# Differential attention: GpSimd combines the softmax pair of the last 256 of 768 keys, VectorE the first 512

## Chip, cores, metric

One NeuronCore of a Trainium2 chip runs the whole kernel in one launch. The metric is the device time of that launch in microseconds (us), lower is better. Names of engines: PE is TensorE (PEld its weight load), DVE is VectorE, ACT is ScalarE, POOL is GpSimd, SP is SyncE.

## What is computed

The model is two blocks in a row: a two-layer recurrent and attention block, and then two hybrid layers over 512 latent tokens and 256 context tokens. Each hybrid layer has three branches; the change is in the first, differential attention. Cut to what matters:

```python
def diff_attn_dense(q, k, v, lam):
    s = jnp.einsum('bqhcd,bkhcd->bhcqk', q, k).astype(jnp.float32) * (q.shape[-1] ** -0.5)
    p = jax.nn.softmax(s, axis=-1)
    a = (p[:, :, 0] - lam * p[:, :, 1]).astype(v.dtype)
    return jnp.einsum('bhqk,bkhv->bqhv', a, v)
```

There are 4 heads. Each has two score maps (c = 0 and 1) with 64 channels each, whose softmaxes are subtracted, the second times lam. A latent query sees all 768 keys, a context query the 256 context keys.

## The kernel before

The kernel is written engine by engine: each engine has one program that walks through the same list of stages, and semaphores, named in the code, order them. Nothing is rescheduled, so the order within an engine is the order of the code.

The stage `da` (differential attention) comes once in each of the two hybrid layers. It is cut into jobs. A latent job is one head and one block of 128 queries: two score maps of 128 x 768. A context job is one head and both context blocks: four maps of 128 x 256. Layer 0 has 20 jobs (for each head four latent ones, then one of context), layer 1 has 16, all latent; so 32 are latent and 4 of context. A job n passes through:

1. PE, `scores` (L986 latent, L977 context): q times k into three PSUM banks, 0 to 2 for even jobs and 3 to 5 for odd.
2. DVE, `maxima` (L2392): the negated row maxima, from PSUM.
3. ACT, `exps` (L1674): exponentials into the SBUF buffer `DE[:, n % 2]`, with row sums.
4. DVE, `probs`: reciprocals of the sums (L2401), the ratio r (L2404, one column), and then one SCALAR_TENSOR_TENSOR (L2410), e0 = e1 * r + e0, over 768 columns for a latent job, two of 256 for a context job. The common factor 1/sum is left out and put in at step 7.
5. PE, `transposes`: blocks 0 to 3 of e0 (L1001) into bank 6, then, for latent jobs, blocks 4 and 5 (L1006) into bank 7. Ahead of blocks 4 and 5 PE waits on `da_evac` of job n-1, since bank 7 also holds that job's output.
6. ACT, `evac` (L1683, L1687): the transposed blocks to SBUF. PE, `values` (L1020): times v into bank 7.
7. DVE, `evac` (L2418): bank 7 times the reciprocal, to SBUF, which gives `da_evac`.
8. ACT `squares` (L1695 to L1702), DVE `scale` (L2427), PE `turn` (L1029), DVE `post` (L2432): norm, transposition back and gate, once for each head (and again for its context rows).

The order within a turn n of the loop is: PE scores(n+2), values(n-1), transposes(n), turn(n-2); DVE probs(n), post(n-3), maxima(n+2), evac(n-1), scale(n-2); ACT exps(n+1), evac(n), squares(n-1). Two lines at the loop's end prepare the next stage's first weights (L575 on DVE, ahead of the loop, and L594 to L596 on PE behind it). GpSimd has nothing to do in `da`: before, it went from the two loads of the rotary tables (L2925) to a wait on `da_y`, the stage's last result, ahead of the load of `wg_in` (L2929). Elsewhere it issues loads, and in the stage `mlstm` it computes masks (L2824) and queries (L2833).

The program has a limited number of semaphores. Three that the change touches: `lru_w` counted the eight loads of `LRUW` (L2877); `loaded_pool` counted the load of `ROT` (L2872) and is waited for in `wait_loaded`, which DVE calls before L1965 and PE before its `lru` stage; `ml_w` told the exponential of the rows `WQ` (L1455) to the GpSimd stores of `wrow` (L2939).

Of the kernel before, what the change touches and what calls it, by code (L numbers as in the profile page):

```python
# [11 lines left out]
ALU = mybir.AluOpType  # L12
# [237 lines left out]
def build(nc, x, ctx_in, w8, wb, wm, wf_in, wg_in, params, rows, lru_w, sgu_w, sgu_b, rope, rot, nbias, vlat, mrow, wrow,  # L250
# [203 lines left out]
    def pc(name, i=0):  # L454
# [7 lines left out]
    slot_uses = [len(range(k, n_ml, 4)) for k in range(4)]  # L462
    state_uses = [len(range(k, n_lat, 4)) for k in range(4)]
    in_layer0 = dict(
        da_probs=n_da, da_evac=n_da, da_o=n_da, da_max=n_da, da_half=16, da_scaled=8, da_turned=8, da_rs=8, da_y=8,
        ml_s=n_mu, ml_u=2 * n_lat, ml_c0=n_lat, ml_c=3 * n_lat, ml_masked=n_ml, ml_qs=n_lat, decay=n_ml,
        ml_zm=n_ml, ml_o=n_ml, ml_dens=n_mu, ml_divf=n_mu, ml_divb=n_mu, ml_rs=n_mu, ml_scaled=n_mu,
        ml_turned=n_mu, ml_y=n_mu, ml_w=1, ml_stored=64, ml_rows=1, ml_l=1, ml_ac=1, ml_emc=1,
        bz_silu=6, cv_done=4, gate_mm=2, gate_f=2, gate_cols=2, wg_hi=1, wg_lo=1, wg_loaded=16, bqk=8, cv_scaled=8, rope_loaded=32,
        rope_done=8, na_probs=2 * n_na, na_max=n_na, na_values=n_na, v_stored=16 * 8, v_blocks=16 * 7,  # L470
        **{f"ml_bm{k}": 16 * slot_uses[k] for k in range(4)}, **{f"ml_bw{k}": 16 * state_uses[k] for k in range(4)})
# [22 lines left out]
    def wait_loaded(eng):  # L494

        eng.wait_ge(loaded, 16)
        eng.wait_ge(sem("rows_loaded"), 16)
        for half in x_loaded:
            eng.wait_ge(half, 16)
        eng.wait_ge(loaded_pool, 16)  # L500

    def wait(eng, s, v):

# [257 lines left out]

    def pe_lru(pe, st):

        pe.wait_ge(sem("lru_w"), 16 * 8)
        for m in range(4):
            wait_free(pe, st, m, 0)
        for m in range(4):
            for g in range(2):
                b = (2 * m + g) % 4
                wait_free(pe, st, b, m // 2)  # L770
                pe.matmul(PS[:, b, :], LRUW[:, 4 * g + m, :], XA[:, m, :],
                          start=True, stop=True).then_inc(full[b], 1)
# [193 lines left out]
    def pe_da(pe, st):  # L966
        ly, jobs = st.layer, st.jobs
        nj = len(jobs)

        def scores(j):  # L970
            n, h, p = j["n"], j["h"], 3 * (j["n"] % 2)
            wait_free(pe, st, p, n // 2)
            lo, hi = slice(0, 64), slice(64, 128)
            if j["ctx"]:
                for qb in range(2):
                    for c, r in ((0, lo), (1, hi)):
                        mm = pe.matmul(PS[:, p + c, qb * TC:(qb + 1) * TC], Q[r, h, T + qb * P:T + (qb + 1) * P],  # L977
                                       K[r, h, T:TA], start=True, stop=True, skip_group_check=True)
            else:
                q0 = P * j["qb"]  # L980
                half = sem("da_half")
                for i, (r, b, c0, k0, k1) in enumerate(((lo, p + 1, 0, T, TA), (hi, p + 2, 0, TC, TA),
                                                        (lo, p, 0, 0, T), (hi, p + 1, TC, 0, TC))):
                    if i == 3:
                        pe.wait_ge(half, past("da_half", ly) + sum(not k["ctx"] for k in jobs[:n]) + 1)
                    mm = pe.matmul(PS[:, b, c0:c0 + k1 - k0], Q[r, h, q0:q0 + P], K[r, h, k0:k1], start=True,  # L986
                                   stop=True, skip_group_check=True)
                    if i == 0:
                        mm.then_inc(half, 1)
            mm.then_inc(full[p], 1)  # L990

        def transposes(j):
            n = j["n"]
            pe.wait_ge(sem("da_probs"), past("da_probs", ly) + n + 1)
            wait_free(pe, st, 6, n)
            outs = sum(i["last"] for i in jobs[:max(n - 2, 0)])
            wait(pe, sem("da_y"), past("da_y", ly) + outs)
            e = DE[:, n % 2, :]
            for i in range(4):
                o = i if not j["ctx"] else 2 * (i % 2) + i // 2  # L1000
                mm = pe.transpose(PS[:, 6, o * P:(o + 1) * P], e[:, i * P:(i + 1) * P], IDENT[:, :])  # L1001
            mm.then_inc(full[6], 1)
            wait(pe, sem("da_evac"), past("da_evac", ly) + n)
            if not j["ctx"]:
                for i in range(4, 6):
                    mm = pe.transpose(PS[:, 7, (i - 4) * P:(i - 3) * P], e[:, i * P:(i + 1) * P], IDENT[:, :])  # L1006
                mm.then_inc(full[7], 1)

        def values(j):
            n, h = j["n"], j["h"]  # L1010
            nl = sum(not i["ctx"] for i in jobs[:n + 1])
            pe.wait_ge(freed[6], st["free", 6] + n + 1)
            pe.wait_ge(freed[7], st["free", 7] + nl)
            wait(pe, sem("da_evac"), past("da_evac", ly) + n)
            at = DAT[n % 2]
            for qb in range(1 + j["ctx"]):
                tiles = (4, 5) if j["ctx"] else range(6)
                for i, t in enumerate(tiles):
                    o = i * TC + qb * P if j["ctx"] else i * P
                    mm = pe.matmul(PS[:, 7, qb * P:(qb + 1) * P], at[:, o:o + P], V[:, t, h * P:(h + 1) * P],  # L1020
                                   start=i == 0, stop=i == len(tiles) - 1, skip_group_check=True)
            mm.then_inc(sem("da_o"), 1)

        def turn(j):

            pe.wait_ge(sem("da_scaled"), past("da_scaled", ly) + j["g"] + 1)
            pe.wait_ge(freed[6], st["free", 6] + min(j["n"] + 3, nj))
            for i in range(2 if j["ctx"] else 4):
                mm = pe.transpose(PS[:, 6, i * P:(i + 1) * P], DO[:, j["g"] % 2, i * P:(i + 1) * P], IDENT[:, :])  # L1029
            mm.then_inc(sem("da_turned"), 1)  # L1030

        pe.wait_ge(sem("rope_done"), past("rope_done", ly) + 8)
        for b in range(8):
            wait_free(pe, st, b, 0)
        scores(jobs[0])
        scores(jobs[1])
        for n in range(nj + 2):
            if n + 2 < nj:
                scores(jobs[n + 2])
            if 0 <= n - 1 < nj:  # L1040
                values(jobs[n - 1])
            if n < nj:
                transposes(jobs[n])
            else:
                pe_head(pe, st.merge, n - nj)
            if 0 <= n - 2 < nj and jobs[n - 2]["last"]:
                turn(jobs[n - 2])
        if st.merge.ctx:
            pe_head(pe, st.merge, 2)
# [343 lines left out]
    def act_units(act, own, st):  # L1393
# [4 lines left out]
        for u, ev in enumerate(st.evs):  # L1398
# [46 lines left out]
            elif ev in ("bq", "bk"):  # L1445
# [5 lines left out]
                if ev == "bk":  # L1451
                    act_gates(act, own, st)
                else:
                    act.wait_ge(sem("ml_rows"), past("ml_rows", st.layer) + 1)
                    act.activation(WQ[0:8, :, :], WQ[0:8, :, :], ACT.Exp).then_inc(sem("ml_w"), 1)  # L1455
                for m in range(4):
                    w = 4 * (8 * st.layer + c0 + m)
                    wait_unit(act, st, u, m, st.ctx)
# [920 lines left out]
    def dve_da(dve, own, st):  # L2379
# [3 lines left out]
        def sums(j, i, at=16):  # L2383
            c = at + 4 * (j["n"] % 4) + i
            return SMALL[:, c:c + 1]
# [9 lines left out]
        def probs(j):  # L2395
            n, p = j["n"], 3 * (j["n"] % 2)
            e = DE[:, n % 2, :]
            dve.wait_ge(freed[p], st["free", p] + n // 2 + 1)
            nq, w = (2, TC) if j["ctx"] else (1, TA)
            c = 4 * (n % 4)  # L2400
            own.link(dve.reciprocal(SMALL[:, 64 + c:64 + c + 2 * nq], SMALL[:, 16 + c:16 + c + 2 * nq]))  # L2401
            for i in range(nq):
                r = SMALL[:, 32 + 4 * (n % 2) + i:33 + 4 * (n % 2) + i]
                own.mark(dve.scalar_tensor_tensor(out=r, in0=sums(j, i), scalar=sums(j, nq + i, 64),  # L2404
                                                  in1=LAM[:, ly, 1:2], op0=ALU.mult, op1=ALU.mult))
            own.wait()
            for i in range(nq):
                r = SMALL[:, 32 + 4 * (n % 2) + i:33 + 4 * (n % 2) + i]
                e0, e1 = e[:, i * w:(i + 1) * w], e[:, (nq + i) * w:(nq + i + 1) * w]
                ins = dve.scalar_tensor_tensor(out=e0, in0=e1, scalar=r, in1=e0, op0=ALU.mult, op1=ALU.add)  # L2410
            ins.then_inc(sem("da_probs"), 1)

# [443 lines left out]
    def _(pool):  # L2856
# [17 lines left out]
        for g in range(2):  # L2874
            for half in range(2):
                for q in range(2):
                    pool.dma_start(LRUW[64 * half:64 * half + 64, 4 * g + 2 * q:4 * g + 2 * q + 2,  # L2877
                                        64 * half:64 * half + 64],
                                   lru_w[g, half, :, 2 * q:2 * q + 2, :]).then_inc(sem("lru_w"), 16)
        pool.wait_ge(w_ready[1], 16)  # L2880
        for i in range(2):
            pool.dma_start(mod_slab(i), wm[i, :, :, :]).then_inc(mod_loaded[i], 16)
        for st in stages:
# [50 lines left out]
                    pool.dma_start(mrow[st.layer, 4 * d:4 * d + 4, :], m_[4 * d:4 * d + 4, :]).then_inc(  # L2934
                        sem("ml_stored"), 16)
            if st.kind == "units" and "bo" in st.evs:
                pool.wait_ge(sem("ml_w"), past("ml_w", st.layer) + 1)
                for d in range(2):
                    pool.dma_start(wrow[st.layer, 4 * d:4 * d + 4, :], WQ[4 * d:4 * d + 4, d, :]).then_inc(  # L2939
                        sem("ml_stored"), 16)  # L2940
# [8 lines left out]
                pool_queries(pool, next_st, next_st.passes[0])  # L2949
            if st.kind == "mlstm":  # L2950
                pool_mlstm(pool, st)

            def bias(ly, i):

# [202 lines left out]
```

## Time and profile before

| | |
|---|---|
| median of 3 runs | 3112.86 us (3111.77 to 3113.13) |
| the profiled execution: its time, its span | 3115.25 us, 3113.5 us |
| busy: PE / DVE / ACT / POOL | 96% / 48% / 37% / 5% of the span |
| stage `da`, layer 0 (first scores to the last `values`) | 1371.9 to 1459.9 us |
| stage `da`, layer 1 | 2413.1 to 2486.0 us |
| chain that ended last, by engine | PE 84%, DVE 9%, ACT 3% |

The profile's busy share is an average over the whole program; the two `da` stages are 161 us of it. In them neither PE nor DVE is busy all the time, so the chain of waits (followed back from the last instruction to what released each step) is what tells which instruction's length counts. Times in the rows further down are us from the span's start.

### The profile page before, as it was taken

What the parts mean: (1) busy time and instruction counts of PE and PEld (TensorE: products, weight loads), DVE (VectorE), ACT (ScalarE), POOL (GpSimd) and SP (SyncE); (2) the same over time, 40 slices, a digit from 0 to 9 for tenths busy, and PEclk for the clock granted to TensorE, in tenths of its full rate; (3) what the DMA queues carried; (4) which work ended last, traced back from release to release, by engine and by line L of the source; (5) the groups of instructions that cost most, each with busy time, mean ns of one, the idle gap of its engine ahead of it and who ended that gap; (6) DMA issues with size and microseconds to landing.
All of it is one profiled execution on the core that took longest, in us unless ns stands there. A gap on an engine that the chain in (4) does not pass through costs nothing.

```text
span 3113.5 us, 38501 instructions
## 1 busy us (share of the span) xinstructions
PE 2975.4 (96%) x15486; PEld 2424.6 (78%) x15486; DVE 1497.5 (48%) x2136; ACT 1155.9 (37%) x1828; POOL 147.6 (5%) x206
## 2 busy tenths in 40 slices
PE   7999999999999998989999999999999899999998
PEld 5767888777788887867888878868877678888776
DVE  4645454645454657267252542263444735353454
ACT  4335233425352344136233331163221634251352
POOL 1000000010000000000000400100000000120100
PEclk9999999999999999999999999999999999999999
DMA  4232322331332221110211211211111022222322
GB/s 178 95 142 101 122 108 101 113 122 68 109 107 91 97 90 54 68 48 4 74 42 62 90 67 54 95 59 61 54 61 68 21 77 67 90 88 81 112 75 81
DMA packets 44460, 256.79 MB, mean 82 GB/s; under 512 B 6344, under 2 KB 6352, under 8 KB 20512
## 3 DMA queue, kind: packets, MB, share of 16 engines
q1 hardware_dynamic: 30528, 204.30, 18.5%
q0 software_dynamic: 13792, 50.51, 5.0%
q8 instruction: 102, 1.67, 0.2%
q14 instruction: 38, 0.31, 0.0%
HBM read 250.51 MB, written 4.28 MB: 82 GB/s over the span
## 4 chain that ended last, share of the span: by engine, by line
PE 84%; DVE 9%; ACT 3%; issue 1%; DMA 1%; POOL 1%; DVEq 0%; SPq 0%; ACTq 0%
PE PS L805 13%; PE PS L806 13%; PE PS L807 13%; PE PS L786 7%; PE PS L785 7%; PE PS L787 7%; PE PS L751 2%; PE PS L750 2%; PE PS L749 2%; DVE SMALL L2392 2%; PE PS L986 1%; DMA W<-in_w 1%; PE PS L698 1%; PE PS L594 1%; PE PS L596 1%
## 5 line engine op out<-in xcount | busy, mean ns | idle before, releaser
L805 PE MATMUL PS<-HHX,WHX 128*128 128x512 f32 (+1 forms) x1456 | 511.2, 351 | 9.9 <-DVE WLX L2242 7.0
L806 PE MATMUL PS<-HL,WHX 128*128 128x512 f32 (+1 forms) x1456 | 512.3, 352 | 0.0
L1559 ACT ACTIVATE WHX<-W 128x2048 fp32r<-128x2048 f32 (+1 forms) x102 | 174.6, 1712 | 578.9 <-DMA W<-in_w 391.3
L807 PE MATMUL PS<-HHX,WLX 128*128 128x512 f32 (+1 forms) x1024 | 357.6, 349 | 0.0
L2242 DVE TENSOR_TENSOR WLX<-W,WHX 128x2048 fp32r<-128x2048 f32 x60 | 137.5, 2292 | 383.4 <-ACT WHX L1559 383.4
L805 PEld LDWEIGHTS PS<-HHX,WHX 128*128 128x128 f32 x1456 | 278.8, 191 | 48.4 <-DVE WLX L2242 7.8
L806 PEld LDWEIGHTS PS<-HL,WHX 128*128 128x128 f32 x1456 | 277.5, 191 | 36.6
L786 PE MATMUL PS<-HL,WH 128*128 128x512 f32 x672 | 265.4, 395 | 0.0
L785 PE MATMUL PS<-HH,WH 128*128 128x512 f32 x672 | 263.3, 392 | 0.0
L2242 DVE TENSOR_TENSOR WL<-W,WH 128x2048 fp32r<-128x2048 f32 x68 | 155.9, 2292 | 221.7 <-ACT WH L1559 221.6
L787 PE MATMUL PS<-HH,WL 128*128 128x512 f32 x672 | 261.7, 389 | 0.0
L1559 ACT ACTIVATE WH<-W 128x2048 fp32r<-128x2048 f32 x68 | 130.3, 1916 | 282.4 <-PE PS L787 252.1
L807 PEld LDWEIGHTS PS<-HHX,WLX 128*128 128x128 f32 x1024 | 196.0, 191 | 24.7
L2280 DVE SCALAR_TENSOR_TENSOR ARENA<-PS,PC,ARENA 128x511 f32<-128x511 f32 (+1 forms) x176 | 131.6, 748 | 73.1 <-ACT ARENA L1587 60.0
L2242 DVE TENSOR_TENSOR WLM<-W,WHX 128x1024 fp32r<-128x1024 f32 (+1 forms) x42 | 70.6, 1680 | 179.2 <-ACT WHX L1559 179.1
L807 PE MATMUL PS<-HHX,WLM 128*128 128x512 f32 (+1 forms) x432 | 154.9, 359 | 0.0
L785 PEld LDWEIGHTS PS<-HH,WH 128*128 128x128 f32 x672 | 125.8, 187 | 30.8
L787 PEld LDWEIGHTS PS<-HH,WL 128*128 128x128 f32 x672 | 126.1, 188 | 28.2
L786 PEld LDWEIGHTS PS<-HL,WH 128*128 128x128 f32 x672 | 126.2, 188 | 27.2
L749 PE MATMUL PS<-WHX,HHX 128*128 128x512 f32 x288 | 119.6, 415 | 0.0
L751 PE MATMUL PS<-WHX,HL 128*128 128x512 f32 x288 | 112.7, 391 | 0.0
L750 PE MATMUL PS<-WLX,HHX 128*128 128x512 f32 x288 | 112.5, 391 | 0.0
(533 smaller groups left out, 5902.4 us busy)
## 6 DMA issues: line engine op xcount, KB each, us to landing
W<-in_w SPq DMA_DIRECT2D x172, 1024.0 KB, 4.7
XC<-in_wm POOLq DMA_DIRECT2D x12, 1024.0 KB, 5.1
H<-in_wm POOLq DMA_DIRECT2D x12, 1024.0 KB, 5.7
W<-in_wb SPq DMA_DIRECT2D x24, 512.0 KB, 3.2
W<-in_w SPq DMA_DIRECT2D x8, 768.0 KB, 4.1
ARENA<-mrow POOLq DMA_DIRECT2D x12, 256.0 KB, 4.1
ARENA<-wrow POOLq DMA_DIRECT2D x12, 256.0 KB, 4.6
PR<-in_nbias POOLq DMA_DIRECT2D x12, 256.0 KB, 2.9
```

The costliest lines, as they stand in the source:

```text
L749: pe.matmul(PS[:, t, :], xh, wh[:, s, c], start=s == 0 and k == 0, stop=False)
L750: pe.matmul(PS[:, t, :], xh, wl[:, s, c], start=False, stop=False)
L751: mm = pe.matmul(PS[:, t, :], xl, wh[:, s, c], start=False, stop=s == 1 and k == 3)
L785: pe.matmul(PS[:, b, :], WH[:, s, c], hi(k), start=k == 0, stop=False)
L786: pe.matmul(PS[:, b, :], WH[:, s, c], lo(k), start=False, stop=False)
L787: mm = pe.matmul(PS[:, b, :], WL[:, s, c], hi(k), start=False, stop=k == kb - 1)
L805: pe.matmul(dst, wh[:, s, c], hi[:, k, t0:t1], start=k == 0, stop=False)
L806: pe.matmul(dst, wh[:, s, c], lo[:, k, t0:t1], start=False, stop=False)
L807: mm = pe.matmul(dst, wl[:, s, c], hi[:, k, t0:t1], start=False, stop=k == kb - 1)
L1559: act.activation(dst[:, s, 0:n], W[:, s, 0:n], ACT.Copy).then_inc(wh_ready[s], 1)
L2242: dve.tensor_tensor(lo[:, s, 0:n], W[:, s, 0:n], hi[:, s, 0:n].bitcast(F32), ALU.subtract).then_inc(wl_ready[s], 1)
L2280: ins = dve.scalar_tensor_tensor(out=CB[:, m, d:T], in0=PS[:, m, 0:T - d], scalar=PC[:, bass.ds(i * 16 + (base + 4 * m + 2 - d), 1)], in1= ...
```

## The change

For latent jobs DVE's SCALAR_TENSOR_TENSOR takes the first 512 columns alone. GpSimd takes columns 512 to 767 in two instructions: a TENSOR_SCALAR, e1 = e1 * r, and, after a wait on its own semaphore, a TENSOR_TENSOR, e0 = e0 + e1. Context jobs stay with DVE. The ratio r now raises the semaphore `da_ratio`, for which both DVE (in the place of its own step semaphore) and GpSimd wait. `da_far` counts GpSimd's two instructions, and PE waits for it ahead of blocks 4 and 5, behind its wait on `da_evac`. To have semaphores for this, the `LRUW` loads now count on `loaded_pool` (waited for at 9 loads rather than 1), and the exponential of `WQ` counts on `ml_l` (waited for at 2).

```diff
-        eng.wait_ge(loaded_pool, 16)
+        eng.wait_ge(loaded_pool, 16 * 9)
...
-        pe.wait_ge(sem("lru_w"), 16 * 8)
+        pe.wait_ge(loaded_pool, 16 * 9)
...
             wait(pe, sem("da_evac"), past("da_evac", ly) + n)
             if not j["ctx"]:
+                pe.wait_ge(sem("da_far"), past("da_far", ly) + 2 * sum(not k["ctx"] for k in jobs[:n]) + 2)
                 for i in range(4, 6):
...
-                    act.activation(WQ[0:8, :, :], WQ[0:8, :, :], ACT.Exp).then_inc(sem("ml_w"), 1)
+                    act.activation(WQ[0:8, :, :], WQ[0:8, :, :], ACT.Exp).then_inc(sem("ml_l"), 1)
...
-                own.mark(dve.scalar_tensor_tensor(out=r, in0=sums(j, i), scalar=sums(j, nq + i, 64),
-                                                  in1=LAM[:, ly, 1:2], op0=ALU.mult, op1=ALU.mult))
-            own.wait()
+                ins = dve.scalar_tensor_tensor(out=r, in0=sums(j, i), scalar=sums(j, nq + i, 64),
+                                               in1=LAM[:, ly, 1:2], op0=ALU.mult, op1=ALU.mult)
+            ins.then_inc(sem("da_ratio"), 1)
+            dve.wait_ge(sem("da_ratio"), past("da_ratio", ly) + n + 1)
             for i in range(nq):
                 r = SMALL[:, 32 + 4 * (n % 2) + i:33 + 4 * (n % 2) + i]
-                e0, e1 = e[:, i * w:(i + 1) * w], e[:, (nq + i) * w:(nq + i + 1) * w]
+                near = w if j["ctx"] else T
+                e0, e1 = e[:, i * w:i * w + near], e[:, (nq + i) * w:(nq + i) * w + near]
                 ins = dve.scalar_tensor_tensor(out=e0, in0=e1, scalar=r, in1=e0, op0=ALU.mult, op1=ALU.add)
...
-                pool.wait_ge(sem("ml_w"), past("ml_w", st.layer) + 1)
+                pool.wait_ge(sem("ml_l"), past("ml_l", st.layer) + 2)
...
+            if st.kind == "da":
+                ly = st.layer
+                for j in st.jobs:
+                    n = j["n"]
+                    if j["ctx"]:
+                        continue
+                    pool.wait_ge(sem("da_ratio"), past("da_ratio", ly) + n + 1)
+                    r = SMALL[:, 32 + 4 * (n % 2):33 + 4 * (n % 2)]
+                    e0, e1 = DE[:, n % 2, T:TA], DE[:, n % 2, TA + T:2 * TA]
+                    pool.tensor_scalar(e1, e1, r, None, ALU.mult).then_inc(sem("da_far"), 1)
+                    nl = sum(not k["ctx"] for k in st.jobs[:n])
+                    pool.wait_ge(sem("da_far"), past("da_far", ly) + 2 * nl + 1)
+                    pool.tensor_tensor(e0, e0, e1, ALU.add).then_inc(sem("da_far"), 1)
```

On GpSimd, between the rotary tables of layer 0 and its load of `wg_in`, the program before has these rows (each name in brackets is a semaphore waited for):

```order
L2925 DMA ARENA<-in_rope 128x512 [waits h_ready]
L2925 DMA ARENA<-in_rope 128x512
L2929 DMA ARENA<-in_wg_in 128x464 [waits da_y]
```

and the changed one begins there with these, 16 pairs in each layer, ahead of `wg_in`:

```order
L2928 DMA ARENA<-in_rope 128x512 [waits h_ready]
L2928 DMA ARENA<-in_rope 128x512
L2964 TENSOR_SCALAR ARENA<-ARENA,SMALL 128x256 [waits da_ratio]
L2967 TENSOR_TENSOR ARENA<-ARENA 128x256 [waits da_far]
L2964 TENSOR_SCALAR ARENA<-ARENA,SMALL 128x256 [waits da_ratio]
L2967 TENSOR_TENSOR ARENA<-ARENA 128x256 [waits da_far]
```

So the 64 new instructions stand where GpSimd had none. On PE, at the first two jobs of layer 0, the changed program has (L1007 are blocks 4 and 5, L1021 the values, one line further down than before):

```order
L1001 MATMUL PS<-IDENT,ARENA 128x128 [waits freed6,da_probs]
L1001 MATMUL PS<-IDENT,ARENA 128x128 x3
L1007 MATMUL PS<-IDENT,ARENA 128x128 [waits da_far]
L1007 MATMUL PS<-IDENT,ARENA 128x128
L986 MATMUL PS<-ARENA 128x256 [waits freed3]
L986 MATMUL PS<-ARENA 128x512 x2
L986 MATMUL PS<-ARENA 128x256 [waits da_half]
L1021 MATMUL PS<-ARENA 128x128 [waits freed7,freed6]
L1021 MATMUL PS<-ARENA 128x128 x5
L1001 MATMUL PS<-IDENT,ARENA 128x128 [waits freed6,da_probs]
L1001 MATMUL PS<-IDENT,ARENA 128x128 x3
L1007 MATMUL PS<-IDENT,ARENA 128x128 [waits da_far,da_evac]
```

No PE instruction has moved. Ahead of blocks 4 and 5 job 0 had no wait of its own and now has one; the later jobs wait for a second semaphore beside `da_evac`.

## Rows read from the trace of the kernel before

**Rows 1.** Groups of DVE by line and shape: busy us, mean ns | idle before.
```profile
L2410 DVE SCALAR_TENSOR_TENSOR ARENA<-ARENA,SMALL 128x768 f32<-128x768 f32 x32 | 32.6, 1019 | 1.1
...
L2410 DVE SCALAR_TENSOR_TENSOR ARENA<-ARENA,SMALL 128x256 f32<-128x256 f32 x8 | 3.5, 482 | 0.1
```

**Rows 2.** Chain of waits, layer 0 of `da`: start us, us, what (x: how many instructions).
```profile
1379.58 1.02 DVE ARENA L2410
...
1382.63 1.02 DVE ARENA L2410
1383.65 1.67 DVE SMALL L2392
...
1393.15 0.44 PE PS L1006 x2
1393.59 1.51 PE PS L986 x6
...
1395.13 1.76 DVE SMALL L2392
1396.89 0.27 DVE PR L2418
```

**Rows 3.** Chain of waits, layer 1 of `da`.
```profile
2424.84 1.67 DVE SMALL L2392
...
2477.95 1.02 DVE ARENA L2410
...
2479.78 0.64 PE PS L1001 x4
```

**Rows 4.** Timeline of DVE, layer 1: start, us, engine, line, operation [idle before <-releaser].
```profile
2430.92 0.22 DVE L2404 SCALAR_TENSOR_TENSOR SMALL<-SMALL,LAM 128x1 f32<-128x1 f32 x1
...
2432.84 1.76 DVE L2392 TENSOR_REDUCE SMALL<-PS 128x2 f32<-128x1536 f32 x1 [0.65 <-PE PS L986]
2434.52 0.34 DVE L2418 TENSOR_SCALAR PR<-PS,SMALL 128x128 f32<-128x128 f32 x1
...
2445.81 1.76 DVE L2392 TENSOR_REDUCE SMALL<-PS 128x2 f32<-128x1536 f32 x1 [0.21 <-PE PS L986]
```

**Rows 5.** Timeline of GpSimd at the start of the program.
```profile
3.37 0.29 POOL L2866 TENSOR_SCALAR_AFFINE_SELECT IDENT<-IDENT 128x128 f32<-128x128 f32 x1 [0.23 <-POOL ARENA L2864]
3.62 1.09 POOL L2868 TENSOR_SCALAR_AFFINE_SELECT SELP<-SELP 8x1024 f32<-8x1024 f32 x1
```

**Rows 6.** Timeline of GpSimd, stage `mlstm`: first of its TENSOR_TENSORs, one alone on 256 columns.
```profile
1654.78 1.29 POOL L2824 TENSOR_TENSOR RST<-RST,MASKS 128x512 f32<-128x512 f32 x1 [2.71 <-DMA RST<-mrow]
...
1789.54 0.72 POOL L2824 TENSOR_TENSOR ARENA<-ARENA,MASKS 128x256 f32<-128x256 f32 x1 [1.41 <-DMA ARENA<-mrow]
```

**Rows 7.** Timeline, stage `na`: a DVE instruction and the GpSimd load that it releases.
```profile
2044.26 0.17 DVE L2475 TENSOR_SCALAR SMALL<-SMALL 128x2 f32<-128x2 f32 x1
...
2044.72 0.54 POOL L2955 DMA_DIRECT2D PR<-in_nbias  x1 [3.46 <-DVE SMALL L2475]
```

**Rows 8.** Timeline, stage `mlstm`: DVE and GpSimd both reading two SBUF operands.
```profile
1769.37 1.82 POOL L2833 TENSOR_TENSOR ARENA<-ARENA 128x512 f32<-128x512 f32 x1
1769.38 0.69 DVE L2696 TENSOR_TENSOR ARENA<-ARENA,SMALL 128x512 f32<-128x512 f32 x1 [2.35 <-ACT SMALL L1846]
...
2733.26 1.84 DVE L2696 TENSOR_TENSOR ARENA<-ARENA,SMALL 128x512 f32<-128x512 f32 x1 [2.34 <-ACT SMALL L1846]
2733.26 1.27 POOL L2833 TENSOR_TENSOR ARENA<-ARENA 128x512 f32<-128x512 f32 x1
```

**Rows 9.** One line's instructions (L2641, one operand in PSUM): duration ns min/median/max.
```profile
L2641 DVE SCALAR_TENSOR_TENSOR ARENA<-PS,ARENA x18: 678/683/687, 1758.3 to 2749.3; 128x512 f32<-128x512 f32 x18
```

**Rows 10.** One line's instructions: the loads of `LRUW`, and DVE's first behind `wait_loaded`.
```profile
L2877 POOL DMA_DIRECT2D ARENA<-in_lru_w x8: 610/622/645, 5.6 to 9.7; - x8
...
DMA to landing us min/median/max: 6.0/6.7/7.2
...
L1965 DVE TENSOR_TENSOR RST<-PR x1: 418/418/418, 76.2 to 76.2; 128x256 f32<-128x256 f32 x1
```

More of the change, by code:

```diff
@@ L464, in build @@
     in_layer0 = dict(
-        da_probs=n_da, da_evac=n_da, da_o=n_da, da_max=n_da, da_half=16, da_scaled=8, da_turned=8, da_rs=8, da_y=8,
+        da_probs=n_da, da_ratio=n_da, da_far=32, da_evac=n_da, da_o=n_da, da_max=n_da, da_half=16, da_scaled=8, da_turned=8, da_rs=8, da_y=8,
         ml_s=n_mu, ml_u=2 * n_lat, ml_c0=n_lat, ml_c=3 * n_lat, ml_masked=n_ml, ml_qs=n_lat, decay=n_ml,
         ml_zm=n_ml, ml_o=n_ml, ml_dens=n_mu, ml_divf=n_mu, ml_divb=n_mu, ml_rs=n_mu, ml_scaled=n_mu,
-        ml_turned=n_mu, ml_y=n_mu, ml_w=1, ml_stored=64, ml_rows=1, ml_l=1, ml_ac=1, ml_emc=1,
+        ml_turned=n_mu, ml_y=n_mu, ml_stored=64, ml_rows=1, ml_l=2, ml_ac=1, ml_emc=1,
         bz_silu=6, cv_done=4, gate_mm=2, gate_f=2, gate_cols=2, wg_hi=1, wg_lo=1, wg_loaded=16, bqk=8, cv_scaled=8, rope_loaded=32,
@@ L2878, in _ @@
                                         64 * half:64 * half + 64],
-                                   lru_w[g, half, :, 2 * q:2 * q + 2, :]).then_inc(sem("lru_w"), 16)
+                                   lru_w[g, half, :, 2 * q:2 * q + 2, :]).then_inc(loaded_pool, 16)
         pool.wait_ge(w_ready[1], 16)
```

## The prediction, made before the changed kernel had run

> **What bounds the kernel now.** I read the chain of waits first, over the two `da` stages, because the change touches nothing else of any length. It has 32 latent SCALAR_TENSOR_TENSORs of 1019 ns [rows 1], but only 5 of the pieces of the chain are L2410: the jobs 0 and 1 of layer 0 (of 1.02 us each [rows 2]), the same two in layer 1, and job 14 there [rows 3]. Everywhere else the chain goes round a loop without it: blocks 4 and 5 of the transposes (0.44), the next scores (1.51), the maxima (1.76), DVE's evacuation (0.27), and again blocks 4 and 5 [rows 2]. That loop takes some 4.05 us a job. The reader is to see that `probs` runs beside the first two of these: DVE evacuates, does reciprocal, ratio and L2410, and then still sits idle 0.65 us until PE's scores are there [rows 4]. Where a `scale` and a `post` stand beside them it is less, but latent maxima still waited 0.21 us for PE [rows 4]. So DVE is no bound in the loop; it is one only while the pipeline fills, where PE's scores were issued early, and once as it drains.
>
> The second view is the timeline of one turn, for the time that GpSimd has. The ratio ends at 2430.92 + 0.22 = 2431.14, the evacuation of job n-1 at 2434.52 + 0.34 = 2434.86, and only then may PE start blocks 4 and 5 [rows 4]. GpSimd's pair must be done within these **3.7 us** to cost nothing.
>
> **DVE's part.** L2410 (L2413 in the changed file) took 482 ns on 256 columns and 1019 on 768 [rows 1], which is 1.049 ns a column; 512 columns then take 482 + 268 = 750 ns, 0.27 less. Over 32 jobs that is 8.6 us of DVE's time. On the path it is 5 x 0.27 = 1.35 us at most; the other 27 times it lengthens the idle time ahead of the maxima. The ratio's wait is one semaphore in place of another: nothing.
>
> **GpSimd's part, alone.** The trace of before has no TENSOR_SCALAR on GpSimd. The nearest rows with one SBUF input are the AFFINE_SELECTs, 0.29 us on 128 columns and 1.09 on 1024 [rows 5]: by the line between them 0.40 us on 256. The bounds are 0.29 below and 0.72 above, as for the two inputs. The TENSOR_TENSOR on 256 columns took 0.72 [rows 6]. GpSimd began 0.29 us after the end of the DVE instruction that released it (2044.43 to 2044.72) [rows 7], and 0.23 us after its own semaphore [rows 5]. In sum 0.29 + 0.40 + 0.23 + 0.72 = 1.64 us from the end of the ratio.
>
> **The two together.** Both engines are released by the ratio, and both then read two SBUF operands or want to. The trace shows what comes of that: started at the same moment as a 512-column TENSOR_TENSOR of DVE that kept its 0.69 us, GpSimd's took 1.82 where it takes 1.27; and in another place DVE's took 1.84, with GpSimd's at its 1.27 [rows 8]. One of the two stood still while the other worked. DVE's reads of PSUM with one SBUF operand never did (678 to 687 ns over 18 [rows 9], some of them beside GpSimd's), so the maxima and the evacuation are safe. DVE's L2410 starts 0.03 us behind the ratio, GpSimd 0.29 behind, so I take DVE to be first: L2410 runs from 0.03 to 0.78, GpSimd's product from 0.78 to 1.18, its sum from 1.41 to 2.13, and PE is released at about **2.17 us**. By the Trainium skill (SBUF — State Buffer, "SBUF: two separate sides") the pair of ports that both share is an exclusive lock for a whole instruction of whichever starts first, also against a DVE instruction with two SBUF inputs where GpSimd's reads SBUF. The rows agree. This rule speaks against the change: without it the pair would be ready at 1.64 and the whole 1.35 us would come back, with it the start of the stage gives its share away, as worked out next.
>
> In the loop 2.17 stands against 3.7: hidden, with 1.5 us to spare; the shortest way from a ratio to the evacuation's end, at job 1 of each layer, where the maxima wait for nothing, is 0.78 + 1.67 + 0.27 = 2.7 [rows 2], and holds too.
>
> **Where it is not hidden: job 0.** There blocks 4 and 5 waited for nothing but blocks 0 to 3, and the scores of job 3 stand behind them on PE's queue, and DVE's maxima(3) behind those. Layer 0: the ratio ends at 1379.56 (the start of L2410 at 1379.58 [rows 2], less the gap). PE starts blocks 4 and 5 at 1379.56 + 2.17 = 1381.73, ends them 0.44 later, the scores 1.51 later, at 1383.68; with 0.03 to DVE, maxima(3) start at 1383.71. By DVE alone they would start at 1383.65 - 0.54 = 1383.11; before it was 1383.65 [rows 2]. So the gain of 0.54 turns into a loss of 0.06. Layer 1 has the same turn, with maxima(3) at 2424.84 [rows 3]: 0.06 again. At job 14 of layer 1 the L2410 is 0.27 shorter, L2432 and blocks 0 to 3 come 0.27 earlier (2479.51); the pair is ready at 2477.92 + 2.17 = 2480.09, blocks 4 and 5 would start at 2479.95 and now start 0.14 later, still ahead of the 0.61 that ACT needs for blocks 0 to 3. So 0.27 stays. **Sum: 2 x 0.06 - 0.27 = -0.15 us.**
>
> **The other edits** go together. The `LRUW` loads are issued from 5.6 to 9.7 us and land within 7.2, at about 17; DVE's first instruction behind `wait_loaded` is at 76.2 [rows 10]: nothing, and if that cover were gone, a microsecond or so once. The `WQ` exponential gives the same event under another name. GpSimd's queue: the 32 pairs stand ahead of the load of `wg_in`, which waited for the stage's end anyhow, and behind loads issued long before; no DMA moves.
>
> The sum is against the profiled execution's 3115.25 us (span 3113.5), which lies 2.4 above the median of the runs, 3112.86. Taken off the median: 3112.7.
>
> **Rivals.**
> (a) **GpSimd first at the port.** Then its product holds DVE up by some 0.40 us and L2410 ends at about 1.20 behind the ratio, 0.15 later than before. Five times on the path: +0.8 us, 3113.6. The idle 0.21 us or more of the loop hides the rest. For it: DVE's was the one that stood still at 2733.26 [rows 8]. Against: the 0.26 us by which DVE starts ahead. Chance 0.12.
> (b) **No stall at all**, both read at once, or the product is quick enough: the full -1.35, 3111.5. For it: L2833 and L2696 at 1769.37 are recorded as starting within 0.01 us [rows 8], so the records don't show who reads when, and the stall may come only in some cases. Chance 0.10.
> (c) **GpSimd becomes the bound: slower.** The price is in `transposes`, at PE's wait on `da_far`: each us by which the pair ends later than 3.7 behind the ratio is paid by each of the 32 latent jobs, since scores, maxima and evacuation stand behind it in the loop. It decides from a pair of 3.7 us on, and would pass 0.2% (6.2 us) at 3.9. With both instructions as long as the stalled one of 512 columns, 1.82 us [rows 8], the pair ends at 0.29 + 1.82 + 0.23 + 1.82 = 4.16 and costs 32 x 0.46 = 15 us: 3127. Against: these have half the columns, and only the first of them can meet L2413. Chance 0.03.
> (d) **A slow first TENSOR_SCALAR.** An instruction of a kind that GpSimd hasn't run may start slowly once; X us of it at job 0 shift that stage by X + 0.06. Its first TENSOR_TENSOR took 1.29 us, as the later ones [rows 6], so the rows give X = 0; as an upper bound I take the stalled 1.82 [rows 8], hence 3114.5. Chance 0.03. By the Trainium skill (GPSIMD Engine Reference, "Instruction dispatch") the first call to a freshly loaded kernel pays some 6 us more; with that the time would be about 3118.6. No run here shows it.
> (e) **DVE bounds the loop after all: faster.** All 32 x 0.27 = 8.6 us, 3104.3. Against it are the idle times of [rows 4]. Chance 0.02.
>
> **How the numbers follow.** The forecast, -0.15 us or, for a reader, no change, has 0.70. A measurement of this kernel can tell about 0.2%, 6.2 us, from no change. Within it lie the forecast, (a), (b) and (d): 0.95. Faster is (e), 0.02; slower is (c), 0.03. The range: the cases (a) and (b) reach from 3111.5 to 3113.6; the runs shown spread over 1.4 us around their median, and the profiled one stood 2.4 above it, which I add above and nearly so below: 3110.3 to 3115.6.
>
> **What would show it.** In the changed profile: L2413 on 512 columns at 750 ns; GpSimd's product recorded at about 0.9 us in the loop (its stall counted in) and its sum at 0.72; DVE's idle ahead of the maxima at 0.9 in place of 0.65; no L2413 in the chain but at jobs 1 and 14; blocks 4 and 5 released by GpSimd at job 0 of each layer, and by DVE's evacuation elsewhere; each stage as long as before within 0.3 us. It is wrong if PE waits for GpSimd in the loop, if the maxima or the evacuation grow, or if L2413 takes over 0.8 us.

## The result, and the profile after

| | before | changed |
|---|---|---|
| median of 20 runs each | 3115.03 us (3111.61 to 3121.38) | 3119.73 us (3114.18 to 3127.63) |
| ratio to before | | 1.0015, 95% interval 1.0008 to 1.0022 |
| profiled execution: span | 3113.5 us | 3118.7 us |
| mean granted TensorE clock | 0.988 | 0.983 |

The changed kernel is slower by 4.7 us or 0.15%, with an interval of 2.5 to 6.9 us. That is within the 0.2% that the prediction called no change, but clear of zero, and above its range. (The 20 runs of before have a median 2.2 us above that of its first three.) One execution of experiment 11 took 5961.7 us and is left out of its ratio as a slow one.

First, the groups of the changed profile by line and shape (busy us, mean ns | idle before, releaser); the first answers to [rows 1]:

```profile
L2413 DVE SCALAR_TENSOR_TENSOR ARENA<-ARENA,SMALL 128x512 f32<-128x512 f32 x32 | 24.1, 752 | 1.1
```
```profile
L2964 POOL TENSOR_SCALAR ARENA<-ARENA,SMALL 128x256 f32<-128x256 f32 x32 | 47.3, 1479 | 340.8 <-DVE SMALL L2405 340.8
L2967 POOL TENSOR_TENSOR ARENA<-ARENA 128x256 f32<-128x256 f32 x32 | 23.3, 727 | 2.7
```

DVE's part is 752 ns where 750 was forecast. GpSimd's product is recorded at 1.48 us every time, where about 0.9 was forecast with its stall, and its sum at 0.73. In the loop this is hidden: the maxima of layer 1 (timeline of DVE, to be held against [rows 4]) still wait for PE, 0.92 us in place of 0.65, and still come every 4.05 us:

```profile
2432.91 1.76 DVE L2393 TENSOR_REDUCE SMALL<-PS 128x2 f32<-128x1536 f32 x1 [0.92 <-PE PS L986]
...
2436.96 1.76 DVE L2393 TENSOR_REDUCE SMALL<-PS 128x2 f32<-128x1536 f32 x1 [0.92 <-PE PS L986]
```

What changed is the start of the stage. The chain of waits in layer 0 (start us, us, what), beside [rows 2]:

```profile
1377.30 0.23 DVE SMALL L2405
1377.53 0.09 issue
1377.62 1.49 POOL ARENA L2964
1379.12 0.07 issue
1379.19 0.73 POOL ARENA L2967
1379.92 0.04 issue
1379.97 0.44 PE PS L1007 x2
1380.41 2.50 PE PS L986 x6
1382.91 2.14 PE PS L1021 x12
...
1387.00 1.53 PE PS L1021 x12
...
1388.98 0.44 PE PS L1007 x2
1389.42 1.51 PE PS L986 x6
```

At job 0 the chain now goes from the ratio through both instructions of GpSimd to PE. The pair ends 2.4 us behind the ratio. But the larger thing is behind it: the same scores (L986) that take 1.51 us in the last line shown take 2.50 there, and the values (L1021) 2.14 where they take 1.53. The windows of the same stretch (us; busy of PE, PEld, DVE, ACT and POOL; PEclk, DMA share, GB/s) say why:

```profile
1371.50:1377.00 5.50, 2.81 (x16) 1.77 (x12) 5.50 (x4) 3.64 (x8) 0.00 (x0) 1.00 0.01 2
1377.00:1380.00 3.00, 0.69 (x5) 0.46 (x5) 2.93 (x6) 0.60 (x1) 2.21 (x2) 1.00 0.44 147
1380.00:1382.00 2.00, 2.00 (x9) 1.40 (x10) 1.01 (x3) 1.56 (x4) 1.52 (x2) 0.68 0.72 303
1382.00:1384.00 2.00, 2.00 (x10) 1.35 (x7) 1.04 (x1) 0.59 (x2) 0.69 (x1) 0.50 0.00 0
1384.00:1386.00 2.00, 1.99 (x17) 1.59 (x17) 1.55 (x5) 0.47 (x1) 0.13 (x1) 0.96 0.00 0
```

The granted clock falls to 0.50, from 2.4 to 1.2 GHz, 0.8 us after PE gets back to work behind a stretch in which it was busy for 0.69 of 3 us, and for nearly all of 1384 to 1386 it is back. In layer 1 there is a fall too, but another one:

```profile
2416.79:2422.00 5.21, 2.74 (x16) 1.78 (x12) 5.21 (x4) 3.42 (x7) 0.00 (x0) 0.98 0.01 3
2422.00:2424.00 2.00, 0.56 (x4) 0.35 (x3) 1.93 (x5) 0.23 (x2) 1.08 (x1) 0.50 0.36 61
2424.00:2426.00 2.00, 1.42 (x8) 0.72 (x6) 1.93 (x4) 0.60 (x1) 1.42 (x3) 0.50 0.74 303
2426.00:2428.00 2.00, 2.00 (x8) 1.50 (x8) 0.38 (x1) 1.96 (x5) 1.90 (x2) 0.50 0.38 160
```
```profile
2422.92 1.49 POOL ARENA L2964
```

The clock is at 0.50 from 2421.8 on (0.98 over 5.21 us is some 0.2 us at half), near the end of the scores that PE does behind its stand for the first exponentials. GpSimd's first instruction of the stage (chain of waits) starts 1.1 us after that, and PE begins to wait for GpSimd only at 2424.8. So this fall can't come from that wait: up to there PE had stood just as in the kernel before. I call such a fall **early**, and one like that of layer 0, which comes in the wait for GpSimd or behind it, **late**.

In the profile of before, PE stood still there too, for 2.47 us for the first exponentials and 1.85 for the first probs, but the clock stayed at 1.00 (timeline of PE, and a window):

```profile
1377.25 1.56 PE L986 MATMUL PS<-ARENA 64*128 64x256 f32 x8 [2.47 <-ACT ARENA L1674]
1380.66 0.66 PE L1001 MATMUL PS<-IDENT,ARENA 128*128 128x128 f32 x4 [1.85 <-DVE ARENA L2410]
1381.15 0.38 PE L1006 MATMUL PS<-IDENT,ARENA 128*128 128x128 f32 x2
1381.46 1.56 PE L986 MATMUL PS<-ARENA 64*128 64x256 f32 x8
```
```profile
1380.00:1382.00 2.00, 1.34 (x10) 1.13 (x12) 2.00 (x2) 0.65 (x2) 0.00 (x0) 1.00 0.79 229
```

For all profiles I use two measures that the timelines give directly. The **stage** is the time from the start of the first maxima to PE's first matmul of the next stage (L594). The **head** is the time from the first maxima to those of job 3. These are the fourth maxima of the stage; the timeline shows those of jobs 0 and 1 in one row, and the expectations below, which count rows, call them the third. A head without a fall of the clock has one length in each kernel, so a fall is seen in it at once.

| | stage, layer 0 / 1 | head, layer 0 / 1 |
|---|---|---|
| before | 86.16 / 71.04 | 10.03 / 10.03 |
| changed | 88.08 / 73.05 | 11.46 / 12.07 |

The two stages together are 3.9 us longer, inside the interval of the whole. The rest of the program took 2956.3 us before and 2957.6 after.

So the theories to be told apart were: **theory 1**, GpSimd's late pair at job 0 makes PE stand longer, and the clock falls behind that; **theory 2**, the other edits or the shifted program; **theory 3**, chance, since falls of the clock are seen all over the program in both profiles; and, as a rival for the mechanism inside theory 1, contention or GpSimd's work as such. For an early fall theory 1 can't hold; the question for it is only how often it comes.

### The profile page after: what moved, and what is told of

It reads as the page before. It is cut to its first block, busy times and chain, and to the rows that moved or that the text cites. A ratio compares the mean times of both kernels' runs of the same rounds, so it can differ in the third digit from the quotient of the medians.

```text
span 3118.7 us, 38596 instructions
## 1 busy us (share of the span) xinstructions
PE 2982.8 (96%) x15486; PEld 2430.2 (78%) x15486; DVE 1489.7 (48%) x2136; ACT 1155.9 (37%) x1828; POOL 219.5 (7%) x270
## 4 chain that ended last, share of the span: by engine, by line
PE 85%; DVE 9%; ACT 3%; issue 1%; DMA 1%; POOL 1%; DVEq 0%; SPq 0%; ACTq 0%
PE PS L805 13%; PE PS L806 13%; PE PS L807 13%; PE PS L786 7%; PE PS L785 7%; PE PS L787 7%; PE PS L751 2%; PE PS L750 2%; PE PS L749 2%; DVE SMALL L2393 1%; PE PS L986 1%; DMA W<-in_w 1%; PE PS L698 1%; PE PS L594 1%; PE PS L1079 1%
```

## The experiments

Only the parts of each diff that matter are shown. The ratios are to before on the same chip.

**1. The other edits alone.** DVE combines all columns, GpSimd nothing.

```diff
-                pe.wait_ge(sem("da_far"), past("da_far", ly) + 2 * sum(not k["ctx"] for k in jobs[:n]) + 2)
...
-                near = w if j["ctx"] else T
+                near = w
...
-            if st.kind == "da":
...
```

> Only the semaphore edits (loads of LRUW counted on loaded_pool, the exponential of WQ on ml_l, the ratio on da_ratio); DVE combines all 768 columns, GpSimd has nothing, PE waits for nothing new. Theory 1 (the loss comes from PE's wait for GpSimd at job 0 of each layer, and from the TensorE clock that falls behind it): same as before within 0.05%, the clock in the first 15 us of both attention stages 1.00. Theory 2 (the loss comes from the other edits or from a shifted program): +3 to +5 us, with the attention stages as long as before. Theory 3 (the loss is only chance in how the clock falls elsewhere): anywhere from -3 to +5 us.

Measured: ratio 1.0000 (0.9991 to 1.0009). Theory 2 falls. But the profile showed something that I had not expected: stages of 87.51 and 71.04 us, heads of 11.35 and 10.04. With no PE instruction changed and no wait for GpSimd, the clock fell at the head of layer 0:

```profile
1378.00:1384.00 6.00, 3.53 (x16) 2.17 (x12) 5.96 (x6) 3.64 (x8) 0.00 (x0) 0.84 0.01 3
1384.00:1386.00 2.00, 1.18 (x6) 0.87 (x5) 1.97 (x3) 0.00 (x0) 0.00 (x0) 0.50 0.51 102
1386.00:1388.00 2.00, 2.00 (x9) 1.49 (x9) 1.93 (x4) 1.72 (x5) 0.00 (x0) 0.50 1.00 422
```

So a fall doesn't need the wait for GpSimd. But this one is early: the clock fell 4.1 us after the first maxima, while the first scores behind the exponentials ran (they took 2.58 us in place of 1.56), and 1.7 us ahead of the ratio. PE had stood for 2.47 us just before, as it does in every profile without idle transposes there.

**2. Job 0 on DVE alone**, the other 30 latent jobs split as in the change.

```diff
-                pe.wait_ge(sem("da_far"), past("da_far", ly) + 2 * sum(not k["ctx"] for k in jobs[:n]) + 2)
+                if far_on(n):
+                    pe.wait_ge(sem("da_far"), past("da_far", ly) + 2 * sum(not k["ctx"] and far_on(k["n"]) for k in jobs[:n]) + 2)
...
-                near = w if j["ctx"] else T
+                near = w if j["ctx"] or not far_on(n) else T
...
+    def far_on(n):
+
+        return n > 0
```

> The change, but job 0 of each layer combined by DVE alone, with no wait of PE for GpSimd there; the other 30 latent jobs as in the change. Theory 1: the clock stays at 1.00 at the start of both stages, each stage is 1.5 to 2 us shorter than in the change, and the whole is the same as before or up to 1 us faster. Theory 2: as the change, +3 to +5 us. A third theory, that the loss is spread over the jobs by GpSimd's pair or by contention: the stages lose 30/32 of what they lost in the change, some 3.6 us.

Measured: 1.0000 (0.9991 to 1.0009). The loss can't be seen any more while 30 of 32 jobs are still split, so it isn't spread over the jobs. Stages 85.91 and 72.57, heads 9.77 and 11.59: 9.77 is before's 10.03 less the 0.27 of job 1's shorter instruction; in layer 1 there was again an early fall, 4.9 us after the first maxima, though no new wait. The forecast of no fall in either was wrong. The third theory asked for some 3.6 us more than before; the interval ends at 2.8.

**3. A wait without reads.** DVE combines everything, GpSimd writes zeros into a spare buffer, and PE waits for the last at job 0.

```diff
+                if n == 0:
+                    pe.wait_ge(sem("da_far"), past("da_far", ly) + 8)
...
+                pool.wait_ge(sem("da_ratio"), past("da_ratio", st.layer) + 1)
+                for i in range(8):
+                    if i:
+                        pool.wait_ge(sem("da_far"), past("da_far", st.layer) + i)
+                    pool.memset(SPARE[:, :], 0.0).then_inc(sem("da_far"), 1)
```

> DVE combines all 768 columns. At job 0 of each layer GpSimd writes zeros eight times to a spare buffer, one after another, from the ratio on, and PE waits for the last ahead of blocks 4 and 5: a wait of the same length as the change's (some 2.3 us behind the ratio) with no reads of SBUF by GpSimd and no other split. Theory 1: PE idle about 0.8 us there, clock 0.5 behind it for some us, each stage about 1.5 to 2.3 us longer than before, the whole +3 to +5 us. If contention at the SBUF port were the cause: stages longer by 0.3 us at most, clock 1.00.

Measured: 1.0003 (0.9994 to 1.0013), which can be told neither from no change nor from the lower end of the forecast. The eight took 2.04 us and PE stood 0.38 us in layer 0 and 0.48 in layer 1, half of the change's 0.95: shorter than meant. Stages 86.31 and 72.72, heads 10.15 and 11.41: a fall in layer 1 alone, where theory 1 had forecast two. It is a late one, behind the stand (timeline of PE, layer 1):

```profile
2421.15 0.41 PE L1009 MATMUL PS<-IDENT,ARENA 128*128 128x128 f32 x2 [0.48 <-POOL SPARE L2962]
2421.49 2.77 PE L987 MATMUL PS<-ARENA 64*128 64x256 f32 x8
```

**4. The change, and PE kept at work in the wait.** Ten transposes into a bank that is overwritten afterwards; the wait for GpSimd is the same.

```diff
+                if n == 0:
+                    for i in range(10):
+                        pe.transpose(PS[:, 7, 0:P], e[:, 0:P], IDENT[:, :])
                 pe.wait_ge(sem("da_far"), past("da_far", ly) + 2 * sum(not k["ctx"] for k in jobs[:n]) + 2)
```

> The change, and at job 0 of each layer PE does 10 further transposes of block 0 into the still unused bank 7, behind blocks 0 to 3, where it waits for GpSimd; their results are overwritten. Theory 1: PE waits as long for GpSimd, but isn't idle, the clock stays at 1.00, and each stage is longer than before by at most 0.5 us (0.26 late pair, less 0.27 in layer 1's tail); the whole within 1 us of before. If the wait alone were the cost, and not the clock: the change's stages, about 1.9 us longer than before each.

Measured: 0.9998 (0.9987 to 1.0008), stages 86.61 and 71.43, heads 10.45 and 10.45: no fall. PE gets to job 3 as late as the wait makes it, and no more. This is the run that parts the two prices of the change: the late pair costs 0.45 us in layer 0 and 0.39 in layer 1; the clock costs the other 88.08 - 86.61 = 1.47 and 73.05 - 71.43 = 1.62 us. The ten transposes stand behind the place of an early fall, so they can't have kept one away: that there was none here is chance, and what the run shows is that no late fall came.

**5. The change once more.**

> The change as it is, once more (an empty line more), to see what repeats. Theory 1, in the form that the first runs leave (a longer stand of PE at job 0 makes a fall of the clock there likelier, it isn't sure): third latent maxima at +10.4 us after the first in a layer without a fall and at +11.4 to +12.1 in one with a fall, at least one of the two layers with a fall; the whole +2 to +5 us. If the first result was chance: the whole within 1 us of before.

Measured: 3119.80 us, 1.0017 (1.0008 to 1.0026); stages 88.08 and 72.94, heads 11.51 and 11.39. It repeats, with a fall in both layers, this time both late (9.2 and 9.4 us after the first maxima); theory 3 falls.

**6. Job 0 on DVE, and PE kept at work at the two places where it stood before the change too.**

```diff
+        def fill(count):
+
+            for _ in range(count):
+                pe.transpose(PS[:, 7, 0:P], IDENT[:, :], IDENT[:, :])
+
...
         scores(jobs[1])
+        fill(18)
         for n in range(nj + 2):
             if n + 2 < nj:
                 scores(jobs[n + 2])
+            if n == 0:
+                fill(14)
```

> Job 0 on DVE alone, the other latent jobs split, and PE does 18 idle transposes (of the identity, into bank 7, overwritten later) where it waits for the first exponentials and 14 where it waits for the first probs. Theory 1: no fall of the clock in the first 20 us of either stage; third maxima at +9.8 us; stages of 85.9 and 70.5 us; the whole 0 to 3 us faster than before, since before falls there in some executions. Rival (the falls do not hang on PE's standing still there): a fall in at least one layer, as in two of the three other kernels with PE idle there.

Measured: 0.9992 (0.9983 to 1.0001); stages 85.90 and 70.74, heads 9.76 and 9.77, as expected: no fall. Once more (experiment 11): 0.9996 (0.9987 to 1.0005), stages 85.92 and 70.76, heads 9.77 and 9.77.

> The split kernel with job 0 on DVE and filled heads once more, to narrow its interval beside the two others on the same chip: stages of 85.9 and 70.7 us, the whole 1 to 3 us faster than before, 0.5 us faster than the filled kernel before and 1 us faster than the filled change.

The stages came out so, the whole did not: its median, 3115.07 us, is 0.9 us below before's, and 3.3 us above that of the filled change (experiment 10), where it should have been 1 us below.

**7. The product behind DVE's instruction.** GpSimd waits for `da_probs`, so the two never meet.

```diff
-                    pool.wait_ge(sem("da_ratio"), past("da_ratio", ly) + n + 1)
+                    pool.wait_ge(sem("da_probs"), past("da_probs", ly) + n + 1)
```

> The change, but GpSimd's product starts behind DVE's SCALAR_TENSOR_TENSOR (it waits for da_probs), so that the two can't meet. If the product's 1.48 us is a stall behind DVE (0.68) and its own work: 0.80 us now, the sum 0.73, and the pair ends as late as before, 2.4 us behind the ratio. If it is all its own work: 1.48 us again, and the pair ends at 3.1 us behind the ratio, so that the third maxima come 0.7 us later than in the change.

The line's instructions in this profile (duration ns min/median/max, first and last start us, form), and the first pair in the timeline:

```profile
L2964 POOL TENSOR_SCALAR ARENA<-ARENA,SMALL x32: 923/925/927, 1378.5 to 2487.2; 128x256 f32<-128x256 f32 x32
```
```profile
1378.53 0.93 POOL L2964 TENSOR_SCALAR ARENA<-ARENA,SMALL 128x256 f32<-128x256 f32 x1 [148.22 <-DVE ARENA L2413]
1379.54 0.72 POOL L2967 TENSOR_TENSOR ARENA<-ARENA 128x256 f32<-128x256 f32 x1
```

Alone the product takes 0.925 us, in the change 1.479: a stall of 0.55 us on each of 32, with DVE's at 752 ns untouched. Neither of the two numbers expected came out: DVE's instruction ends 0.68 us after GpSimd's begins, and 0.13 us of GpSimd's own 0.925 passed beside it. The pair ends 0.2 us later than in the change, not 0.7. One execution took 3119.12 us, with falls in both layers (stages 88.28 and 74.73, heads 12.05 and 12.36): late in layer 0, early in layer 1. The ports' lock, which the Trainium skill states (SBUF — State Buffer, "SBUF: two separate sides"), is seen in the change: DVE, first by 0.07 us, lost nothing, and GpSimd waited. By that page the second engine fully blocks; here all but 0.13 us of GpSimd's work did.

**8. The pure wait, longer**: as 3, with 16 memsets.

> As the timer, with 16 memsets in place of 8: PE waits some 2.3 us longer at job 0 of each layer, GpSimd reads nothing. By the wait alone each stage gets 2.3 us longer than with 8 (third maxima at +12.4). Theory 1: the clock falls at both heads, and each stage is longer by another 1 to 2 us.

Timeline of PE, layer 0, and a window of it:

```profile
1379.63 0.66 PE L1002 MATMUL PS<-IDENT,ARENA 128*128 128x128 f32 x4 [1.85 <-DVE ARENA L2415]
1382.78 0.69 PE L1009 MATMUL PS<-IDENT,ARENA 128*128 128x128 f32 x2 [2.49 <-POOL SPARE L2962]
1383.40 2.93 PE L987 MATMUL PS<-ARENA 64*128 64x256 f32 x8
1386.26 2.72 PE L1023 MATMUL PS<-ARENA 128*128 128x128 f32 x12
```
```profile
1384.00:1386.00 2.00, 2.00 (x8) 1.19 (x4) 0.00 (x0) 1.65 (x4) 0.00 (x0) 0.50 0.00 0
```

One execution took 3121.86 us. Heads 13.87 and 13.94, stages 91.01 and 75.52: the clock fell in both layers, and here GpSimd read nothing and DVE combined all columns. In layer 0 the fall is late, and began while PE still stood. Against the 8 memsets with no fall (layer 0, 86.31) the stage is 4.7 us longer where the wait is 2.1 longer; the other 2.6 is the clock. A stall of PE alone can bring a late fall, here and in layer 1 of experiment 3. Layer 1 had an early fall, 5.1 us after the first maxima, and says nothing on the wait.

**9. Before, filled** at the two places of experiment 6, with nothing else.

> The kernel before (no split, no other edit) with the 18 and 14 idle transposes of PE at the start of both stages. Theory 1 (the clock at the stage's start is what moves the time, the split itself brings 0.3 us a stage at most): no fall at either head, stages of 86.2 and 71.0 us, the whole 0 to 2.5 us faster than before, and within 1 us of the split kernel with the same filling. If the split were worth something: that one is faster than this by more than 1 us.

Measured: 1.0000 (0.9989 to 1.0011); stages 86.19 and 71.04, heads 10.04 and 10.04. No fall at the heads, as expected, but no gain of the whole that can be told from nothing. On the same chip the split kernel with the same filling (experiment 11) had a median 1.8 us lower, more than the 1 us that was to speak for the split; but both intervals hold that difference, and the stages of the two differ by 0.5 us together.

**10. The change, filled at all three places**, and once more (experiment 12).

> The change as it is, with PE's idle transposes at all three places (18, 14, and the 10 ahead of the wait for GpSimd). Theory 1: no fall at either head, third maxima at +10.4 to +10.5 us, stages of 86.5 and 71.4 us, the whole 0.5 us slower to 2 us faster than before; that is 3 to 6 us faster than the change. If the falls came from GpSimd's work itself: as the change, +3 to +5 us.

Measured: 3111.77 us, 0.9988 (0.9979 to 0.9997); stages 86.61 and 71.45, heads 10.44 and 10.45. PE and GpSimd in this profile's timelines:

```profile
1377.56 1.75 PE L1040 MATMUL PS<-IDENT 128*128 128x128 f32 x14
1379.21 0.66 PE L1001 MATMUL PS<-IDENT,ARENA 128*128 128x128 f32 x4
1379.70 1.26 PE L1007 MATMUL PS<-IDENT,ARENA 128*128 128x128 f32 x10
1380.81 0.44 PE L1010 MATMUL PS<-IDENT,ARENA 128*128 128x128 f32 x2
1381.18 1.56 PE L986 MATMUL PS<-ARENA 64*128 64x256 f32 x8
```
```profile
1378.47 1.48 POOL L2975 TENSOR_SCALAR ARENA<-ARENA,SMALL 128x256 f32<-128x256 f32 x1 [146.86 <-DVE SMALL L2416]
1380.03 0.73 POOL L2978 TENSOR_TENSOR ARENA<-ARENA 128x256 f32<-128x256 f32 x1
```

GpSimd's pair is as long and as late as in the change; the scores behind it take 1.56 us again. So GpSimd's work as such brings no fall. The whole came out further below before than the 2 us expected.

> The filled change once more, to see whether its lead over before repeats. Theory 1: no fall of the clock in the first 20 us of either stage, stages of 86.6 and 71.4 us, third maxima at +10.4; the whole 4 to 7 us below the change's 3119.8. If its first result (0.9988 of before) holds, 2 to 4 us faster than before; by the stages alone it should be 0.8 us slower than a before without falls, so that I expect 0 to 3 us faster.

Measured: 3112.56 us, 0.9993 (0.9984 to 1.0002); stages 86.60 and 71.42, heads 10.45 and 10.44.

**Taken together.** Layers with a fall of the clock at the head, over all profiles. The early falls came 4.1 to 5.1 us after the first maxima, ahead of the ratio in all kernels; the late ones 8.8 to 9.4 us after them. The last column counts only layers that had no early fall.

| PE at the head | profiles | early falls | late falls |
|---|---|---|---|
| stands as before, no wait for GpSimd | before, 1, 2 | 2 of 6 | 0 of 4 |
| stands, and waits for GpSimd too | changed, 3, 5, 7, 8 | 3 of 10 | 6 of 7 |
| stands as before, kept at work in the wait | 4 | 0 of 2 | 0 of 2 |
| kept at work where it stood before, no wait for GpSimd | 6, 9, 11 | 0 of 6 | 0 of 6 |
| kept at work there and in the wait | 10, 12 | 0 of 4 | 0 of 4 |

So the wait for GpSimd adds late falls, 6 of 7 against none of 4, and work for PE in that wait takes them away, none of 6. Early falls come with and without the wait, in 5 of the 18 layers in which PE stood as before. None in the 10 with filled first stands points to filling them, but could be chance.

The change itself had a fall in 4 of 4 layers, three late and one early. Its excess over before is two late pairs, 0.45 + 0.41 = 0.86 us (experiment 10 against before), and late falls of some 1.5 us in the layers that have no early one: as an estimate, 0.86 + 2 x 1.5 x (1 - 5/18) = 3.0 us on average, up to 3.9 as in the two profiles. The measured 4.7 has an interval that begins at 2.5. That the estimate is 1.7 us lower than the measured value isn't explained further.

**What stays open.** The filled change is the fastest kernel of the study, 0.12% and 0.07% below before, though its two stages are 0.86 us longer than before's without falls. So its lead doesn't come from the stages. The rest of the program took 2951.7 and 2951.2 us in its two profiles, 2956.3 in that of before, 2949.9 in experiment 4, and from 2952 to 2962 in the others; the clock falls for a few us at 14 to 17 other places in every profile (windows of 2 us), not always the same ones. The filled change had 14 and 15 of them, before 17; but experiment 11 had 14 too, with 2959.6 us in the rest, so the count alone doesn't explain it. What does wasn't tried. Its first interval lies below 1, the second reaches 1.0002; I would call it as good as before, and 0.2% better than the change. How often before falls at its heads is known from few profiles only, and what decides between an early fall, a late one and none in the same program isn't shown.

## Why the prediction was wrong

- **The bound, and DVE's part**: right. L2413 took 752 ns (750 forecast), DVE's idle time ahead of the maxima grew from 0.65 to 0.92 us, the loop kept its 4.05 us, and no job between the first and the last few felt anything. Of 8.5 us that DVE saved, nothing came through.
- **GpSimd's part, alone**: mis-sized. The product's 0.40 us, by the line between two AFFINE_SELECTs, was 0.925. Even the upper bound, the 0.72 of a two-input instruction, was below it. The second of the two rows had 8 partitions; the trace of before has another AFFINE_SELECT, on 128 partitions, in its groups by line:

```profile
L2891 POOL TENSOR_SCALAR_AFFINE_SELECT ARENA<-ARENA 128x1024 f32<-128x1024 f32 x1 | 3.1, 3096 | 3.7 <-DMA ARENA<-in_sgu_b 3.7
```

  The line from 0.29 at 128 columns to this one gives 0.69 at 256, nearer to the truth; I had taken the wrong neighbour. Two small terms went the other way: GpSimd started 0.09 us behind the ratio, not 0.29 (that row was of a DMA issue), and 0.07 behind its own semaphore, not 0.23. The sum was 0.73, as forecast.
- **The two together**: right in kind. DVE was first and kept its time, so rivals (a) and (b) fell. PE started blocks 4 and 5 at 2.44 us behind the ratio, not 2.17.
- **Job 0**: right in place and mechanism, short in size: 0.41 us at each head in place of 0.06 (experiment 10). Of the missing 0.35, 0.27 is the later start of blocks 4 and 5. Some 0.09 is a reading: the prediction took before's maxima(3) from the chain of waits, 1383.65, where the timeline has them start at 1383.56, since that row begins before the one ahead of it ends.
- **Job 14 of layer 1**: wrong. With the pair 0.2 us later, blocks 4 and 5 became the chain's link there (changed kernel):

```profile
2482.12 1.49 POOL ARENA L2964
2483.61 0.07 issue
2483.68 0.74 POOL ARENA L2967
2484.42 0.14 issue
2484.56 0.41 PE PS L1007 x2
2484.97 0.52 issue
2485.49 1.57 PE PS L1021 x12
```

  and the 0.27 us didn't come. So with its own terms put right the sum would have been the +0.86 of the stages without falls, not -0.15: still no change, 3113.7.
- **The step that failed** is that sum's silence on PE's clock. It priced PE's longer stand at job 0 as a delay and kept every PE duration as it was (0.44, 1.51). [rows 2] had them at full clock, in a stretch where PE had just stood for 2.47 and 1.85 us. With the added 0.95 us (timeline of the changed kernel) the scores took 2.50. Falls of the clock made 3.1 of the 3.9 us in the two stages of the changed profile: 1.47 in layer 0, behind the wait, and 1.62 in layer 1, where the fall was early and the wait had no part in it. In the repeat both falls were behind the wait. None of the rivals held such a cost. The chance of 0.95 given to "within 0.2%" was kept by the size of the loss, not by the reasoning.
- **Rivals (c), (d), (e)**: not borne out. The pair had 1.3 us to spare in the loop, the first TENSOR_SCALAR took 1.48 us like all others, and the loop didn't get shorter.
- **The range** leaned on three runs that spread over 1.4 us. Over 20 runs before spread over 9.8.

## What to carry to other kernels

Where a pipeline fills, PE stands anyhow, and a helper engine put on the way of the first job is paid there, even if it is hidden for every later one: give the first job to the fast engine, or do the split from job 1 on. Price a longer stand of PE twice, as a delay and as matmuls that may run at half clock behind it, above all where the profile shows PE already standing for some us just ahead; and a few matmuls without use, into a bank that is overwritten, took the second price away here (no late fall in 6 layers, against 6 in 7). Before blaming a wait for a fall of the clock, look whether the fall came behind it: one of the two in the changed profile came ahead. Before moving work off an engine, look whether its idle time ahead of its next wait would only grow.

## What the runs showed of the hardware

- A GpSimd TENSOR_SCALAR of 128 x 256 float32 with a per-partition scalar took 0.925 us alone, more than its TENSOR_TENSOR of two full operands, 0.727. DVE does 512 columns of the fused form in 0.752.
- A stall behind DVE's two SBUF operands cost GpSimd 0.55 us of the 0.68 that DVE still needed; some 0.13 us of its work went on beside DVE's.
- The granted clock fell to 0.50 at the head in one of two layers with the same waits (experiments 1 and 2): the same stand of PE cost nothing or 1.4 to 1.8 us. The dearest fall cost some 3.1 us (experiment 7, layer 1, where the clock stayed at 0.50 for some 10 us).
- In the wait for GpSimd or behind it the clock fell in 6 of 7 layers, after stands there of 0.48 to 2.49 us, and in none of 6 with ten transposes of PE in the wait.
